# A first feed-forward whose first two down projections become one product in seven halves, with two more panel buffers and the convolution's taps behind the panel splits

## The reference, cut to what matters

```
hn = rmsnorm(h, norm2_g[l])
up = causal_dwconv(jnp.einsum("bsd,df->bsf", hn, ffn_w_up[l]), ffn_conv_w[l]) + ffn_conv_b[l]
f_gate, f_val = jnp.split(up, [D_FF], axis=-1)
h = h + jnp.einsum("bsf,fd->bsd", jax.nn.silu(f_gate) * f_val, ffn_w_down[l])
```

## Time and profile before

| | |
|---|---|
| median of 3 runs | 2140.8 us (2138.76 to 2141.86) |
| profiled execution | 2137.23 us, span 2135.0 us |
| PE busy | 2118.7 us, 99% of the span |
| DVE busy | 1483.1 us, 69% |
| ACT busy | 1047.9 us, 49% |
| POOL busy | 543.3 us, 25% |
| first feed-forward, chunks 0 to 2 | about 595.8 to 956.4 us of the span |

### The profile page before, as it was taken

How to read it: one execution, slowest core, us unless ns; L and a number is a source line. 1 busy time by engine, 2 the same in 40 slices (tenths; PEclk the granted TensorE clock), 3 DMA queues, 4 the chain that set the end, 5 groups by cost and what they waited for, 6 DMA issues and landing times.

```text
span 2135.0 us, 31735 instructions
## 1 busy us (share of the span) xinstructions
PE 2118.7 (99%) x11828; PEld 1821.1 (85%) x11828; DVE 1483.1 (69%) x2421; ACT 1047.9 (49%) x1851; POOL 543.3 (25%) x450
## 2 busy tenths in 40 slices
PE   9999999999999999999999999999999999999998
PEld 6777898888888888888887899999887778999897
DVE  7768334687578485776777587878666785868775
ACT  6876443436432222253777354554445763545543
POOL 2100431143322021143665231200222222311012
PEclk9999999999999999999999999999999999999999
DMA  8887312444676686533445357995322334555673
GB/s 266 252 242 216 99 57 73 168 158 166 230 195 158 176 190 167 142 105 98 159 176 170 113 177 219 284 259 187 99 96 82 89 74 125 174 183 186 201 194 128
DMA packets 140281, 348.89 MB, mean 163 GB/s; under 512 B 38113, under 2 KB 42465, under 8 KB 126817
## 3 DMA queue, kind: packets, MB, share of 16 engines
q1 hardware_dynamic: 123840, 235.19, 33.8%
q0 software_dynamic: 9360, 68.69, 15.2%
q10 hardware_dynamic: 6928, 42.99, 5.6%
HBM read 333.71 MB, written 115.87 MB: 211 GB/s over the span
## 4 chain that ended last, share of the span: by engine, by line
PE 92%; DVE 3%; ACT 2%; issue 1%; DVEq 0%; POOLq 0%; POOL 0%; DMA 0%; SPq 0%; ACTq 0%
PE bank L422 9%; PE bank L423 9%; PE bank L426 9%; PE bank L542 8%; PE bank L545 8%; PE bank L543 8%; PE bank L935 5%; PE bank L939 5%; PE bank L937 5%; PE bank L441 3%; PE bank L440 3%; PE bank L439 3%; PE bank L2463 1%; PE bank L1729 1%; PE bank L2490 1%
## 5 line engine op out<-in xcount | busy, mean ns | idle before, releaser
L336 ACT ACTIVATE b_wh<-b_raw 128x1024 fp32r<-128x1024 f32 (+2 forms) x313 | 323.0, 1034 | 616.9 <-PE bank L426 341.3
L347 DVE TENSOR_TENSOR b_wl<-b_raw,b_wh 128x1024 fp32r<-128x1024 f32 (+2 forms) x270 | 341.4, 1265 | 111.7 <-ACT b_wh L336 109.0
L542 PE MATMUL bank<-b_xh,b_wh 128*128 128x512 f32 x712 | 295.1, 414 | 0.5 <-DVE b_wl L347 0.4
L543 PE MATMUL bank<-b_xl,b_wh 128*128 128x512 f32 x712 | 278.0, 390 | 0.0
L545 PE MATMUL bank<-b_xh,b_wl 128*128 128x512 f32 x704 | 275.9, 392 | 0.0
L1142 POOL TENSOR_TENSOR b_yl<-b_arena,b_yh 128x512 fp32r<-128x512 f32 x50 | 78.4, 1568 | 589.4 <-ACT b_yh L1053 355.9
L422 PE MATMUL bank<-b_xh,b_wh 128*128 128x512 f32 x504 | 197.2, 391 | 0.1
L423 PE MATMUL bank<-b_xl,b_wh 128*128 128x512 f32 x504 | 196.3, 389 | 0.0
L426 PE MATMUL bank<-b_xh,b_wl 128*128 128x512 f32 x496 | 193.3, 390 | 0.0
L347 POOL TENSOR_TENSOR b_wl<-b_raw,b_wh 128x1024 fp32r<-128x1024 f32 (+1 forms) x45 | 104.0, 2310 | 219.5 <-ACT b_wh L336 187.2
L545 PEld LDWEIGHTS bank<-b_xh,b_wl 128*128 128x128 f32 x704 | 132.1, 188 | 29.3
(11 more groups left out here) (565 smaller groups left out, 5291.4 us busy)
## 6 DMA issues: line engine op xcount, KB each, us to landing
scr_sums<-in_quarters POOLq DMA_DIRECT2D x32, 1024.0 KB, 9.1
scr_sums<-in_quarters ACTq DMA_DIRECT2D x28, 1024.0 KB, 5.0
b_more_raw<-scr_sums SPq DMA_DIRECT2D x108, 256.0 KB, 3.1
b_raw<-scr_sums SPq DMA_DIRECT2D x100, 256.0 KB, 3.4
scr_sums<-scr_sums POOLq DMA_DIRECT2D x20, 1024.0 KB, 8.7
b_raw<-in_quarters SPq DMA_DIRECT2D x80, 256.0 KB, 3.0
b_more_raw<-in_quarters SPq DMA_DIRECT2D x76, 256.0 KB, 3.0
scr_sums<-in_quarters ACTq DMA_DIRECT2D x7, 1536.0 KB, 6.7
```

The source lines that it names most:

```text
L336: act.activation(panel_hi_lo(n)[0][:, cols], raw_of(n)[:, cols], ACT.Copy).then_inc(w_hi, 1)
L347: dve.tensor_tensor(lo, raw_of(n)[:, cols], hi.bitcast(F32), ALU.subtract).then_inc(w_lo, 1)
L542: pe.matmul(bank[:, :], ph[:, w], hi[:, x, :], start=(k == 0), stop=False)
L543: last = pe.matmul(bank[:, :], ph[:, w], lo[:, x, :], start=False, stop=(n in SIDE_BY_SIDE and k == kt - 1))
```

## The change

`c0dn` stays at 8 panels and `c1dn` becomes 20, both worked by `down_seven` as in `s`. Their panels go through four buffers, (2, 3, n % 2, n % 2) in turn; the two new ones lie in the arena. `c0up`, `c1up` and `c2up` keep two buffers. Eight more quarter sums are copied and eight more added (56 each), at other places in the program. `kept_pool` takes the place of `hidden_pool` in `c0up`. DVE gets `down_sum` in `c1up`, `down_parts` in `c1dn` and `add_down` in `c2up`, and loses `add_to_h` in `c0dn` and `c1dn`. In an up chunk the value's taps and product now come behind the panel's split, as the gate's taps did; all of them were on DVE before, too. The diff, cut to its core:

```diff
-        ("c0up", 16, 8), ("c0dn", 8, 8), ("c1up", 16, 8), ("c1dn", 8, 8), ("c2up", 12, 8), ("c2dn", 8, 6),
+        ("c0up", 16, 8), ("c0dn", 8, 8), ("c1up", 16, 8), ("c1dn", 20, 8), ("c2up", 12, 8), ("c2dn", 8, 6),
-DOWN = {f"{l}{ch}dn": names for l in "sm" for ch, names in
+DOWN = {f"{l}{ch}dn": names for l in "csm" for ch, names in
+for _seg in ("c0dn", "c1dn"):
+    for _i in range(CNT[_seg]):
+        _n = BASE[_seg] + _i
+        BUFFER[_n] = (2, 3, _n % 2, _n % 2)[_i % 4]
...
+            if BUFFER[n] >= 2 and n < BASE["fv0"]:
+                i = 2 * (BUFFER[n] - 2)
+                return spare[:, i, :], spare[:, i + 1, :]
...
+        c_raw = take(36 * T, 2, DT * P)
...
+                def value():
+                    taps()
+                    product()
+                    if ch == 1:
+                        for part in range(3):
+                            m = down_sum(dve, l, q, part)
+                        if q == 7:
+                            m.then_inc(sums_lo, 1)
+
+                def gate():
+                    taps().then_inc(gate_conv, 1)
+
+                def convolved():
+                    (gate, value)[r]()
+                    if ch == 2 and t < 10:
+                        add_down(dve, l, t)
+                if l == "c":
+                    return convolved
...
             split_and(dve, split_lo, f"{l}{ch}up", post, True)
+            for n in range(BASE[f"c{ch}dn"] + 2, BASE[f"c{ch}dn"] + 4):
+                if l == "c" and n in DOWN_OF:
+                    split_lo(dve, n, 0, n % 2, KT_OF[n])
...
-                if 0 < t < 6:
+                if t > 0:
                     copy_quarter(act, EARLY + 15 + t, s_copied)
...
+                    else:
+                        m.then_inc(out_free, CNT[f"{l}1dn"] + (CNT[f"{l}0dn"] if l != "c" else 0))
             for ch in range(3):
                 hidden_dve(dve, "c", ch, "norm2" if ch == 0 else None)
-                split_and(dve, split_lo, f"c{ch}dn", add_to_h(dve, "an0", "an0f") if ch == 2 else add_to_h(dve), True)
+                split_and(dve, split_lo, f"c{ch}dn", (None, down_parts, add_to_h(dve, "an0", "an0f"))[ch], ch == 2)
...
-                products_down(pe, f"c{ch}dn", lambda k: (y_ready, YR["c"] + PAIRS[ch][0] + k + 1))
+                if ch < 2:
+                    down_seven(pe, f"c{ch}dn")
+            products_down(pe, "c2dn", lambda k: (y_ready, YR["c"] + PAIRS[2][0] + k + 1))
```

More of the change, by code:

```diff
@@ L445, in down_seven @@
             l, second = seg[0], seg[1] == "1"
-            mid, base = f"{l}1st", BASE[seg]
-            read = SEVEN[mid][2] + SEVEN[mid][3]
+            base, tiles = BASE[seg], DOWN_TILES[l]
+            read = sum(SEVEN[f"{l}1st"][2:4]) if l != "c" else 0
             for i in range(CNT[seg]):
@@ new lines, in build @@
+        second = take(20 * T, 4, T)
+        acc_lo, second_lo = (operands(f"down_lo{i}", arena_at + 4 * at * T, 4, T) for i, at in enumerate((16, 20)))
+        hT01_lo = operands("down_lo2", xl_at + 4 * 4 * T, 4, T)
+        c_tiles = DownTiles("c_down", (acc, second), (acc_lo, second_lo), 24 * T, 28 * T, 30 * T, 32 * T,
+                            [(6, 7), (2, 3), (6, 7), (4, 5), (2, 3), (0, 1), (2, 3)])
+        sm_tiles = DownTiles("down", (acc, hT01), (acc_lo, hT01_lo), ARENA - 4 * T, 36 * T, 0, 2 * T,
+                             [(6, 0), (7, 1), (6, 0), (2, 3), (7, 1), (4, 5), (7, 1)])
@@ L766, in taps, with product @@
                     return conv_taps(dve, scaled, dst, 3, lambda j: V("fconv", c * 3 + j), V("fbias", c))
-                if l == "c" and r == 0:
-                    return lambda: taps().then_inc(gate_conv, 1)
-                if l == "c":
-                    taps()
-                if r == 1:
+                def product():
                     dve.drain()
@@ L832, in hidden_act @@
             if l == "c":
+                for n in range(BASE[f"c{ch}dn"] + 2, BASE[f"c{ch}dn"] + 4):
+                    if n in DOWN_OF:
+                        split_hi(act, n, 0, n % 2, KT_OF[n])
                 product_hi(cnt - 1)
@@ L2924, in _ @@
             for ch in range(3):
+                q0, i0, cnt = ((5, 23, 2), (1, 27, 6), (1, 36, 4))[ch]
+                beside = {q0 + k: lambda i=EARLY + i0 + k: add_sum(pool, i) for k in range(cnt)}
                 if ch == 0:
-                    kept_pool(pool, "s")
+                    kept_pool(pool, "s", beside)
                 else:
-                    hidden_pool(pool, "s", ch, {1 + k: lambda i=EARLY + 25 + k: add_sum(pool, i) for k in range(5)} if ch == 1 else {})
-                for i in (range(EARLY + 23, EARLY + 25), range(EARLY + 30, EARLY + 33), ())[ch]:
+                    hidden_pool(pool, "s", ch, beside)
+                for i in (range(EARLY + 25, EARLY + 27), range(EARLY + 33, EARLY + 36), ())[ch]:
                     add_sum(pool, i)
@@ L2973, in _, with first_banks, down_sums @@
             split_and(act, split_hi, "wout", with_copies)
+            def first_banks(n, t, q, r, bank):
+                l = layer_of(n)
+                if t == 5 and l == "s":
+                    act.wait_ge(r_ang, 1)
+                if t == 5:
+                    act.wait_ge(mm_done, BASE[f"{l}0dn"] + 4)
+                    tiles = DOWN_TILES[l]
+                    for b in range(2):
+                        m = act.activation(tiles.p1[:, b, :], pb[tiles.banks[0][b]][:, :], ACT.Copy)
+                        if l == "c" and b == 0:
+                            m.then_inc(out_free, CNT["c0dn"])
+                        else:
+                            m.then_inc(bank_copied, 2 if l == "c" else 1)
+            def down_sums(n, t, q, r, bank):
+                l = layer_of(n)
+                base, tiles = BASE[f"{l}1dn"], DOWN_TILES[l]
+                if t == 0:
+                    act.wait_ge(mm_done, BASE[f"{l}0dn"] + 8)
+                    for b in range(2):
+                        act.activation(tiles.p7[:, b, :], pb[tiles.banks[1][b]][:, :], ACT.Copy).then_inc(bank_copied, 1)
+                if t == 5:
+                    act.wait_ge(sums_lo, sums_lo0[l] + 1)
+                    act.wait_ge(mm_done, base + 4)
+                if t in (5, 6):
+                    dst, tokens = ((yh, T1), (yl, T0))[t - 5]
+                    for x in range(2):
+                        act.activation(dst[:, 4 * x:4 * x + 4, T0], tiles.kept[x][:, :, tokens], ACT.Copy).then_inc(sums_hi, 1)
+                if t == 9:
+                    act.wait_ge(mm_done, base + 8)
+                    for x in range(2):
+                        act.activation(yl[:, 4 * x:4 * x + 4, T1], tiles.third[:, 4 * x:4 * x + 4, :], ACT.Copy)\
+                            .then_inc(sums_hi, 1)
             act.wait_ge(s_gain, 1)
```

235 lines of the change are left out of this document (113 added, 122 removed).

## The result

The changed kernel takes 2151.16 us in the median of 5 runs (2148.45 to 2152.22), the kernel before 2140.8 (2137.32 to 2141.86): a ratio of 1.0056, 95% interval 1.0045 to 1.0067. The medians lie 10.4 us apart, and by the interval the change costs between 9.6 and 14.3 us; the forecast was 2142.8. Its profiled execution took 2150.93 us, its span is 2149.1.

What follows compares the result with a forecast made beforehand. PE was taken as the bound, with DVE close behind. Matmuls -6.3, `c0dn` entry +1.0, `c1dn` wait +2.4, `c2up` entry +3.9 and clock +1.0 gave +2.0 us: 2139.2 profiled, 2142.8 as median; range 2137.5 to 2147.5.

Steps and rivals of the forecast that it cites:

- The matmuls' gain: In `c0dn` and `c1dn`, the new form's matmuls take 80.7 us instead of 87.0: 6.3 us gained if PE never waits.
- The entry of `c0dn`: PE waits at the start of `c0dn` until DVE has scaled the last bank of `c0up`: +1.0 us.
- The entry of `c2up`: PE's first up panel waits for `out_free`, raised by the last instructions of `down_parts`: +3.9 us, the surest term.
- Loads: ... 0, at most 1: Down panels load 512 KB per 2.88 us, as in `s1dn`, where PE did not wait: 0, at most 1 us.
- two adds more run beside `s0st` ... hidden: Extra copies and adds, two adds of them beside `s0st`, are hidden; if not, some 1 to 2 us.
- The prediction's own signs of being wrong: PE waits inside an up chunk, a split waits for a panel's load, or the second or third feed-forward shows new waits.
- A pair needs 10.8: In `c1up`, DVE needs 10.8 us per pair of panels despite `down_sum`, so PE feels nothing inside the chunk.
- the 0.78 of the held tap: In `c1up`, 0.78 us of DVE's pair is no work and goes as its tap slides behind POOL's instruction.
- +2.4: PE waits 2.3 to 2.4 us at the third panel of `c1dn` for a split behind DVE's remaining work.
- +1.0: The clock falls once behind the new waits of PE, with 2.1 us at half speed: 1.0 us lost.
- VectorE becomes the bound: Rival, 14%: a pair needs 11.6 to 12 us, PE waits in `c1up`, `c1dn` and `c2up`: 2148.
- the clock falls twice: Rival, 12%: PE's clock falls twice and stays down, +4 instead of +1, giving 2145.8.

Runs made afterwards that it cites:

- j: Changed kernel with the six-panel piece of weight sums fourth again instead of sixth, so its adds are 1 MB: 2147.9 us, 1.0044 of the kernel before.
- p: Kernel before the change with one edit, the six-panel piece of weight sums sixth instead of fourth: 2142.5 us, 1.0019 of the kernel before.
- n: Changed kernel with earlier `out_free`, earlier `c1dn` splits, first `c1up` tap on ScalarE, no `c0dn` entry wait, six-panel piece fourth, `s0up` adds later: 2135.5 us.
- k: Changed kernel with all nine adds of weights beside or behind `c1up` moved beside and behind `c2up`: 2184.3 us, 1.0207 of the kernel before.
- r: Like n, but with all taps of `c1up` on VectorE again, as in the changed kernel: 2136.1 us, 0.9989 of the kernel before.
- d: Changed kernel with GpSimd's low part of the hidden tile in `c1up` cut to 8 columns instead of 512: 2144.3 us, 1.0029 of the kernel before.
- e: Changed kernel with the first tap of every `c1up` panel moved from VectorE to ScalarE: 2143.8 us, 1.0025 of the kernel before.

## Why the prediction was wrong

**Right.** The matmuls' gain, 6.3 us. The entry of `c0dn`, 1.0. The entry of `c2up`, 3.9 forecast and 3.7 in every profile in which neither the counter was moved nor the wait filled. The third panel of `c1dn` as the place of a wait and the train behind it. No wait inside `c0up` or `c2up`.

**The step that failed** is "Loads: ... 0, at most 1" together with "two adds more run beside `s0st` ... hidden". I counted the moves, eight more copies and eight more adds, and priced them by `s1dn`, where DMA stood at 0.94 and nobody waited. Three things were wrong with that. The regrouped `PIECES` were in the change, and I did not ask where the six-panel piece's adds would now run. I did not ask either at which point of an add a load would be issued, once the value's split had moved (6.1 us to landing in j, with adds of the old size). And a high DMA share without a wait in one stage says nothing of another: `s1dn` has four buffers, `c1up` two. A buffer is freed by VectorE's split about 2.4 us behind the end of one panel, and its next panel is to be split at the end of the second panel after that, 10.88 us behind the same point: 8.4 us for a load that took up to 9.8, and for ACT's copy of 1.06. The earlier trace rows had `c1up` at a share of 0.62 before; the changed kernel has 0.80, p 0.67. The price was 4.0 us in `c1up`, together with VectorE's lack of room (next paragraph), and 1.0 in `s0st` (0.2 to 2.3 there in the other profiles with these two adds beside `s0up`; n, which moves them, does not have this wait). The prediction's own signs of being wrong all came: PE waits inside `c1up`, a load is what a split waits for, and the second feed-forward has a new wait.

**VectorE in `c1up`: half right.** "A pair needs 10.8" was close for loads on time: 10.9 in k, where it does no harm. The reason given, that the 0.78 of the held tap goes, was wrong: POOL's instruction follows the product by one ACT instruction, so it moves along with VectorE, and in its late state falls on `down_sum` (0.93). The rival with "11.6 to 12" had the right mechanism: 11.33, and 12.0 with a late load. p shows that late loads suffice for as large a loss; k, that VectorE's work without them does no harm to `c1up`. j and r (88.6 and 88.4, 1 MB adds, all taps on VectorE) against n (87.07, one tap less) fit with VectorE enlarging what loads begin; that rests on one profile each. The ratios speak for it: less work for VectorE (d, e) gave back 5.8 and 6.6 us of the kernel, where each also shortened `c1dn` (by 2.6 and 2.0), adds of the old size (j) 2.6. As far as these profiles go, then, the 4.0 us of the changed kernel need both, and neither has a share of its own.

**`c1dn`, a size.** +2.4 was +4.8 (0.9 + 3.6 of idling, and 0.3 of lag): VectorE was 1.9 us late at the last value, not 0.1, and POOL's hold fell into the train. This does not come from the loads: k has waits of 0.48 and 3.56 there although `c1up` took 87.07.

**The clock, a size.** +1.0 was +3.1: both long waits were followed by about 3.3 us at half speed, not one by 2.1. That was a rival too, priced +4.

**The chances.** Two rivals came true at once, "VectorE becomes the bound" (2148) and "the clock falls twice" (2145.8), and I had put them side by side as if one excluded the other. Added onto one another they give 2151; the range ended at 2147.5. That this meets the median is in part luck: the first rival put 2 us of waits into `c1up` and some into `c2up`, and named no load. One slip is in the working: 384 matmuls at 87.00 us for 385 are 86.8 us, not 86.9, which changes nothing. The clock in particular is no case of its own: it rides on whatever makes PE wait long.

## What to carry to other kernels

When a change moves transfers, list per stage what each queue moves before and after, in MB, in the size of one transfer and by the moment of its issue, and hold it against how long a buffer of that stage may be late; a DMA share from a stage with more buffers is no cover. Before a cheaper product is put in, look for the counter that its last instruction raises and for who waits for it: here 5.5 of the 10 us came back in the two stages by raising it two panels earlier. And count a long wait of PE twice, once as idling and once as the slow matmuls behind it.
